# Expert weights of a mixture-of-experts layer consumed in two halves of the inner width

## The chip, the cores and the metric

The kernel runs on one core of one Trainium2 chip. The metric is device time in microseconds of one execution, as the median of three runs. A profile of one further execution gives the times of single instructions and transfers; all times below marked as positions are microseconds from the start of its span.

## What is computed

Two transformer layers over 256 tokens of width 1024, all in float32. Each layer has an attention mixer and then a mixture of 32 experts; a token goes to two experts of one group. The expert part, cut to what matters:

```
for e in range(N_EXPERTS):                       # 32 experts
    h = jax.nn.silu(xt @ w_gate[e]) * (xt @ w_up[e])   # 1024 -> 512, twice
    y = y + combine[:, e:e + 1] * (h @ w_down[e])      # 512 -> 1024
```

`w_gate`, `w_up` and `w_down` are 2 MB for each expert, so a layer's experts are 192 MB and the two layers' 384 MB.

## The kernel before

Experts are worked through in 16 pairs for each layer (`PAIRS`). The tokens of a pair are gathered into `xg` (64 slots for each expert), and the two experts stand side by side on TensorE: expert 0's 64 weight columns in one half of the array, expert 1's in the other, so that two matrix products stream at once. A float32 product shows in the trace as two MATMUL instructions.

The weights of a pair are 12 blocks of 1 MB (`CHUNKS`): four of gate, four of up, four of down, each block with its part of both experts. They lie in a ring of 16 places in SBUF (`places`), with six extra places for once in pair 3 (`once`). From pair 2 on SyncE issues them two at a time, 2 MB each (`two_chunks`), in the order in which TensorE uses them, and each issue waits until TensorE has released the places (`s_used`, `used_before`). `chunk_there` is TensorE's wait for a block.

A pair on TensorE (`pair`): the four gate blocks into PSUM bank 2 and the four up blocks into bank 3 (`up_chunk`, products of 512 columns), then two `scatter` products that add the previous pair's result `ye` to the tokens' sums, four transposes of `hid`, two more scatters, two transposes of `pickw` (the next scatter's selection), and then the four down blocks (`down_chunk`). Beside it ScalarE (`experts`) applies silu to the gate result, copies the next pair's tokens into `xg` in four copies (`ranges`), copies the turned hidden values to `hidT`, and copies half of `ye`; VectorE multiplies the up result by the silu (`hid`), copies `pickT` and the other half of `ye`. The first pair (`first_pair`) and the last (`last_pair`) have orders of their own; the last one puts its scatters between the gate and up blocks, works with `hid` in halves, and reads the last two down blocks column half by column half, so that the result's first half is ready sooner.

Layer 1 here is the first of the two, layer 2 the second. While the last blocks of layer 1 are used, the loads of layer 2's mixer (`w_in`, and `bias` out of `bounce`) are already queued behind them.

## Time and profile before

| | |
|---|---|
| median of 3 runs | 1183.36 us (1182.89 to 1183.46) |
| profiled execution | 1183.12 us, its span 1181.3 us |
| TensorE matmul busy | 1117.4 us (95% of the span) |
| VectorE, ScalarE, GpSimd busy | 237.0, 243.4, 168.5 us |
| read from HBM | 441.49 MB, 375 GB/s over the span |
| TensorE's idle time ahead of gate and up products | 46.2 us, most of it ended by a transfer of up or gate weights |
| mean granted TensorE clock | 0.996 |

The profiled execution is 0.24 us below the median of the runs. Busy times are unions over an engine's instructions; TensorE's ends are modelled, so its share does not say that it is at its peak. What waits for what is read from the idle times in the timeline and from the chain of work that ended last. The expert stages are the stretches from about 154 to 584 us and from about 738 to 1170 us.

### The profile page before, as it was taken

Reading aid. Unit: us, or ns where it says so; the run is one execution under the profiler, and the core shown is the slowest. Engines: PE = TensorE matmul, PEld = TensorE weight load, DVE = VectorE, ACT = ScalarE, POOL = GpSimd, SP = SyncE. Lnnn points to the kernel's source line nnn. Section 1 sums busy time; section 2 is a strip of 40 time slices with the busy share of each in tenths; the row PEclk is TensorE's granted clock in tenths of the full one; section 3 lists DMA queues with packets and bytes.
Section 4 is the critical chain, followed back from the end, with each engine's and each line's share of the span. In section 5 each row is a group of like instructions: output and inputs, shape, how many; then the busy total and the mean of one; then the engine's idle time right before and its main releaser. Section 6 shows DMA issues by size and latency. Waiting matters only on the chain.

```text
span 1181.3 us, 14644 instructions
## 1 busy us (share of the span) xinstructions
PE 1117.4 (95%) x5246; PEld 507.1 (43%) x5246; DVE 237.0 (20%) x637; ACT 243.4 (21%) x568; POOL 168.5 (14%) x347
## 2 busy tenths in 40 slices
PE   8999999999999888889999999999999998888897
PEld 6876543333333332323398856333333333333332
DVE  2864331000000000000145544300000000000002
ACT  2144251111211111111112233411211111111112
POOL 0003011111111111110046510211111111111100
PEclk9999999999999999999999999999999999999999
DMA  7985589999999999999998355899999999999994
GB/s 260 348 333 225 203 318 428 429 426 428 428 426 431 428 428 428 428 427 428 423 353 353 113 209 208 340 429 427 427 427 428 429 427 428 428 429 428 427 429 199
DMA packets 48590, 443.33 MB, mean 375 GB/s; under 512 B 9564, under 2 KB 14744, under 8 KB 16792
## 3 DMA queue, kind: packets, MB, share of 16 engines
q1 hardware_dynamic: 47464, 441.34, 90.0%
q10 hardware_dynamic: 1072, 1.26, 0.3%
q8 instruction: 35, 0.57, 0.2%
q14 instruction: 19, 0.16, 0.0%
HBM read 441.49 MB, written 1.09 MB: 375 GB/s over the span
## 4 chain that ended last, share of the span: by engine, by line
PE 67%; DMA 28%; ACT 2%; DVE 1%; issue 1%; ACTq 0%; SPq 0%; POOL 0%; DVEq 0%; POOLq 0%
PE PS L1671 24%; PE PS L1680 13%; DMA places<-in_moe_w_up 12%; DMA places<-in_moe_w_gate 11%; PE PS L1687 7%; PE PS L1555 5%; PE PS L1361 5%; PE PS L1423 4%; DMA places<-in_moe_w_down 3%; PE PS L1427 2%; PE PS L1435 1%; PE PS L1510 1%; DMA bias<-in_c_rel_bias 1%; PE PS L1539 1%; PE PS L1384 1%
## 5 line engine op out<-in xcount | busy, mean ns | idle before, releaser
L1671 PE MATMUL PS<-places,mix 128*64 128x512 f32 x1984 | 444.2, 597 | 46.2 <-DMA places<-in_moe_w_up 31.3
L1671 PEld LDWEIGHTS PS<-places,mix 128*64 128x64 f32 x1984 | 141.1, 137 | 340.6 <-issue 278.3
L1680 PE MATMUL PS<-places,gain_att 128*64 128x512 f32 x960 | 213.8, 596 | 0.8 <-ACT gain_att L861 0.5
L1687 PE MATMUL PS<-mix 128*128 128x512 f32 x256 | 124.8, 608 | 0.0
L826 ACT ACTIVATE mix<-acts 128x512 f32 x120 | 76.3, 636 | 229.7 <-PE PS L1671 217.3
L1680 PEld LDWEIGHTS PS<-places,gain_att 128*64 128x64 f32 x960 | 65.8, 137 | 124.5 <-issue 122.8
L574 POOL TENSOR_TENSOR sm<-sm 128x1 f32<-128x1 f32 x32 | 6.2, 193 | 692.9 <-PE PS L1762 660.3
L1279 DVE TENSOR_TENSOR mix<-PS,mix 128x512 f32<-128x512 f32 x28 | 19.4, 692 | 420.2 <-PE PS L1671 420.2
L633 POOL TENSOR_SCALAR mix<-drop 128x64 f32<-128x64 f32 x128 | 72.2, 584 | 0.0
L1687 PEld LDWEIGHTS PS<-mix 128*128 128x128 f32 x256 | 43.2, 189 | 60.0 <-issue 60.0
L873 ACT ACTIVATE mix<-PS 128x512 f32<-128x512 f32 x32 | 19.1, 598 | 236.8 <-PE PS L1680 224.9
L853 ACT ACTIVATE mix<-PS 128x512 f32<-128x512 f32 x32 | 19.1, 597 | 209.2 <-PE PS L1671 209.2
L1285 DVE COPY mix<-PS 128x512 f32<-128x512 f32 x32 | 22.1, 691 | 195.4 <-PE PS L1680 185.1
L1423 PE MATMUL PS<-acts,places 128*128 128x256 f32 x224 | 52.3, 386 | 0.0
L1423 PEld LDWEIGHTS PS<-acts,places 128*128 128x128 f32 x224 | 41.4, 190 | 8.3 <-issue 2.9
L1555 PE MATMUL PS<-places,mix 128*128 128x512 f32 x96 | 43.8, 598 | 0.0
L1361 PE MATMUL PS<-acts,places 128*128 128x128 f32 x336 | 40.5, 277 | 0.0
L1361 PEld LDWEIGHTS PS<-acts,places 128*128 128x128 f32 x336 | 38.8, 192 | 0.9 <-issue 0.7
L681 ACT ACTIVATE gain_att<-gain_att,sm 128x128 f32<-128x128 f32 (+1 forms) x64 | 28.5, 447 | 37.8 <-DVE sm L991 37.8
L1281 DVE COPY mix<-PS 128x256 f32<-128x256 f32 x32 | 13.6, 425 | 110.5 <-PE PS L1762 98.1
L690 ACT ACTIVATE gain_att<-PS 128x256 f32<-128x256 f32 (+2 forms) x32 | 14.4, 450 | 61.4 <-PE PS L1510 61.2
L1555 PEld LDWEIGHTS PS<-places,mix 128*128 128x128 f32 x96 | 17.3, 190 | 17.9 <-issue 17.9
(245 smaller groups left out, 801.0 us busy)
## 6 DMA issues: line engine op xcount, KB each, us to landing
places<-in_moe_w_gate SPq DMA_DIRECT2D x56, 2048.0 KB, 25.1
places<-in_moe_w_down SPq DMA_DIRECT2D x54, 2048.0 KB, 32.5
places<-in_moe_w_up SPq DMA_DIRECT2D x52, 2048.0 KB, 30.4
places<-in_moe_w_gate SPq DMA_DIRECT2D x16, 1024.0 KB, 10.9
places<-in_moe_w_up SPq DMA_DIRECT2D x16, 1024.0 KB, 6.5
places<-in_moe_w_down SPq DMA_DIRECT2D x16, 1024.0 KB, 7.4
places<-in_c_w_in SPq DMA_DIRECT2D x12, 1024.0 KB, 20.7
places<-in_ab_w_in SPq DMA_DIRECT2D x8, 1024.0 KB, 14.1
```

Of the source, the lines that this page charges most:

```text
L633: pool.tensor_scalar(pickw[:, t, e * SLOTS:(e + 1) * SLOTS], now_slots, now[:, t, e:e + 1], now_w[:, t, e:e + 1], ALU.is_equal, ALU.mult). ...
L681: act.activation(att[:, u % ATT, j, 0:n], att[:, u % ATT, j, 0:n], ACT.Exp, bias=nmax[:, u % ATT, j:j + 1], accum_out=den[:, 2 * u + j:2 * ...
L826: act.activation(dst[:, blocks, 0:SLOTS], src[:, blocks, 0:SLOTS], ACT.Copy).then_inc(s_xg[l], 1)
L1279: dve.tensor_tensor(hid, PS[:, 3], hid, ALU.mult).then_inc(s_hi[l], 1)
L1285: dve.tensor_copy(ye[:, 512:1024], PS[:, 7]).then_inc(s_yd[l], 1)
L1361: last = mm(PS[:, bank, m * P:(m + 1) * P], held, moved, start=(k == 0), stop=(k == 3))
L1423: last = mm(bank[0:m, half * SEQ:(half + 1) * SEQ], w[:, k, half * P:half * P + m], src[:, k, :], start=(k == 0), stop=(k == NK - 1))
L1427: last = mm(bank[:, half * CW:(half + 1) * CW], src[:, k, half * P:half * P + P], w[:, k, :], start=(k == 0), stop=(k == NK - 1))
L1555: last = mm(PS[:, OUT_BANK[q]], src[:, t * P:(t + 1) * P], wo[:, k // KPC, k % KPC, 512 * b:512 * b + 512], start=(m == 0), stop=(m == NK ...
L1671: last = mm(PS[e * SLOTS:(e + 1) * SLOTS, 2 + part, :], xg[:, k, e * SLOTS:(e + 1) * SLOTS], w[e][:, kk, :], start=(k == 0), stop=(k == NK ...
L1680: last = mm(PS[e * SLOTS:(e + 1) * SLOTS, 6 + b, :], hidT[:, k, e * SLOTS:(e + 1) * SLOTS], w[e][:, 512 * b:512 * b + 512], start=(k == 0) ...
L1687: last = mm(PS[:, Y_BANK[q]], pickT[:, t], ye[:, 512 * b:512 * b + 512], start=first, stop=final)
```

## The change

From the second pair on, the 512 inner columns of a pair are worked in two halves of 256. A half is two gate blocks, two up blocks, then, once its hidden values are made and turned, the two down blocks whose 256 rows belong to it. The weights are laid out anew by the host so that a 1 MB gate or up block holds four row groups of 256 columns instead of two of 512 (`halves`); bytes, transfer sizes and the number of transfers stay. The first pair keeps the old layout, which is appended as a seventeenth entry that only it reads. The last pair has the order of every other, with its last two down blocks still read column half by column half.

```diff
-            def block_of(c):
-                if c < 2 * UP_CHUNKS:
-                    return (w_gate, c) if c < UP_CHUNKS else (w_up, c - UP_CHUNKS)
-                return w_down, c - 2 * UP_CHUNKS
+            def block_of(i, c):
+                if i == 0:
+                    ...
+                return (w_gate, w_up, w_down)[c // 2 % 3], c // 6 * 2 + c % 2
...
 # ScalarE, experts()
-                    act.wait_ge(s_used[l], i * CHUNKS + UP_CHUNKS)
...
-                    if not first and not final:
-
-                        act.wait_ge(s_used[l], i * CHUNKS + 2 * UP_CHUNKS)
+                    for half in range(2):
+                        fs = slice(half * F // 2, (half + 1) * F // 2)
+                        ks = slice(half * NF // 2, (half + 1) * NF // 2)
+                        if not first:
+                            act.wait_ge(s_used[l], i * CHUNKS + half * CHUNKS // 2 + 2)
+                            act.wait_ge(s_ht[l], i * 2)
+                            act.activation(hid[:, fs], PS[:, 2, fs], ACT.Silu).then_inc(s_si[l], 1)
+                        act.wait_ge(s_ht[l], i * 2 + half + 1)
+                        act.activation(hidT[:, ks], PS[:, 2 + half if first else 2, fs].rearrange("p (k n) -> p k n", k=NF // 2),
+                                       ACT.Copy).then_inc(s_hT[l], 1)
+                    if not final:
                         ranges(entries, i * COPIES + FIRST_COPIES)
...
 # VectorE, experts()
+                    for half in range(2):
+                        fs = slice(half * F // 2, (half + 1) * F // 2)
+                        dve.wait_ge(s_used[l], i * CHUNKS + (2 * UP_CHUNKS if first else half * CHUNKS // 2 + 4))
+                        dve.wait_ge(s_si[l], i * 2 + half + 1)
+                        dve.tensor_tensor(hid[:, fs], PS[:, 3, fs], hid[:, fs], ALU.mult).then_inc(s_hi[l], 1)
...
 # TensorE
+                def up_chunk(i, n, rounds, c):
+
+                    half, part, rows = c // 6, c // 2 % 3, NK // 2
...
+                    for kk in range(rows):
+                        k = c % 2 * rows + kk
+                        for e in range(AT_ONCE):
+                            last = mm(PS[e * SLOTS:(e + 1) * SLOTS, 2 + part, half * F // 2:(half + 1) * F // 2],
+                                      xg[:, k, e * SLOTS:(e + 1) * SLOTS], w[e][:, kk, :], start=(k == 0), stop=(k == NK - 1))
...
+                def pair(i, n, rounds=0, second=False, final=False):
+
+                    for half in range(2):
+                        for c in range(6 * half, 6 * half + 4):
+                            up_chunk(i, n, rounds, c)
+                        if half == 0:
+                            ye_there(i - 1)
+                        scatter(2 * half, second)
+                        pe.wait_ge(s_hi[l], i * 2 + half + 1)
+                        for k in range(half * NF // 2, (half + 1) * NF // 2):
+                            last = nc.tensor.transpose(PS[:, 2, k * P:(k + 1) * P], hid[:, k * P:(k + 1) * P], ident)
+                        last.then_inc(s_ht[l], 1)
+                        scatter(2 * half + 1, second)
+                        if half == 1:
+                            pe.wait_ge(s_pw[l], i * PICKS + PICKS)
+                            for t in range(NT):
+                                last = nc.tensor.transpose(PS[:, 3, t * P:(t + 1) * P], pickw[:, t], ident)
+                            last.then_inc(s_pkt[l], 1)
+                        pe.wait_ge(s_hT[l], i * 2 + half + 1)
+                        if not (final and half):
+                            for k in range(half * NF // 2, (half + 1) * NF // 2):
+                                down_chunk(n, rounds, k)
```

How TensorE's instructions stand in one pair (here the second pair of a layer). Before: L1671 are the gate and up products, L1687 the scatters, L1756 and L1762 the transposes of `hid` and `pickw`, L1680 the down products; `xN` counts products (two MATMUL records each, one for a transpose).

```order
L1671 MATMUL PS<-places,mix 64x512 x32
L1687 MATMUL PS<-mix 128x512 x2
L1756 MATMUL PS<-acts,mix 128x128 x4
L1687 MATMUL PS<-mix 128x512 x2
L1762 MATMUL PS<-acts,mix 128x128 x2
L1680 MATMUL PS<-places,gain_att 64x512 x16
```

The same pair of the changed kernel, where L1677 are the gate and up products, L1696 the scatters, L1734 and L1740 the transposes and L1689 the down products:

```order
L1677 MATMUL PS<-places,mix 64x256 x32
L1696 MATMUL PS<-mix 128x512
L1734 MATMUL PS<-acts,mix 128x128 x2
L1696 MATMUL PS<-mix 128x512
L1689 MATMUL PS<-places,gain_att 64x512 x8
L1677 MATMUL PS<-places,mix 64x256 x32
L1696 MATMUL PS<-mix 128x512
L1734 MATMUL PS<-acts,mix 128x128 x2
L1696 MATMUL PS<-mix 128x512
L1740 MATMUL PS<-acts,mix 128x128 x2
L1689 MATMUL PS<-places,gain_att 64x512 x8
```

The 32 gate and up products of 512 columns have become 64 of 256, and each scatter and transpose stands between products of one half; the second half's up blocks are now followed by two scatters, two and two transposes and the last two down blocks.

TensorE at the end of a layer, before: the scatters lie between the blocks of the last pair, and between the last up block and the last two down blocks (L1722) stand the transposes of `hid` (L1707) and `pickw` (L1713) and the first two down blocks (L1680).

```order
L1671 MATMUL PS<-places,mix 64x512 x8
L1687 MATMUL PS<-mix 128x512
L1705 REGISTER_ALU
L1707 MATMUL PS<-acts,mix 128x128 x2
L1705 REGISTER_ALU
L1707 MATMUL PS<-acts,mix 128x128 x2
L1680 MATMUL PS<-places,gain_att 64x512 x4
L1711 REGISTER_ALU
L1713 MATMUL PS<-acts,mix 128x128 x2
L1680 MATMUL PS<-places,gain_att 64x512 x4
L1722 MATMUL PS<-places,gain_att 64x512 x8
L1687 MATMUL PS<-mix 128x512 x4
```

After, from the second half of the last pair on (L1752 are its last two down blocks; REGISTER_ALU rows work out the numbers that waits in the loop compare with):

```order
L1677 MATMUL PS<-places,mix 64x256 x32
L1696 MATMUL PS<-mix 128x512
L1732 REGISTER_ALU
L1734 MATMUL PS<-acts,mix 128x128 x2
L1696 MATMUL PS<-mix 128x512
L1738 REGISTER_ALU
L1740 MATMUL PS<-acts,mix 128x128 x2
L1752 MATMUL PS<-places,gain_att 64x512 x8
L1772 REGISTER_ALU
L1696 MATMUL PS<-mix 128x512 x4
```

The first two down blocks have left the place between the last up block and the last two down blocks, and two scatters have come there.

ScalarE in the second pair, before: silu (L853), four copies of the next pair's tokens (L826, one shown, each with the setting of its address), the copy to `hidT` (L871), half of `ye` (L873).

```order
L853 ACTIVATE mix<-PS 128x512
L826 ISA
L826 ACTIVATE mix<-acts 128x8x64
...
L871 ACTIVATE gain_att<-PS 128x512
L873 ACTIVATE mix<-PS 128x512
```

After: silu (L860) and the copy to `hidT` (L862) once for each half, then the four copies of tokens (L828, one shown), then half of `ye` (L870).

```order
L860 ACTIVATE mix<-PS 128x256
L862 ACTIVATE gain_att<-PS 128x256
L860 ACTIVATE mix<-PS 128x256
L862 ACTIVATE gain_att<-PS 128x256
L828 ISA
L828 ACTIVATE mix<-acts 128x8x64
...
L870 ACTIVATE mix<-PS 128x512
```

The four copies have moved from behind the silu, while TensorE does its scatters, to behind the second half's copy to `hidT`, when only the last two down blocks are left of the pair.

## Rows read from the trace of the kernel before

**Rows 1.** The page's 40 equal slices of the span: GB/s moved.
```profile
GB/s 260 348 333 225 203 318 428 429 426 428 428 426 431 428 428 428 428 427 428 423 353 353 113 209 208 340 429 427 427 427 428 429 427 428 428 429 428 427 429 199
```

**Rows 2.** Windows of one pair: stretch, length, busy by engine, TensorE clock, DMA share, GB/s.
```profile
180.22:205.26 25.04, 25.04 (x113) 8.92 (x111) 1.81 (x4) 4.22 (x7) 2.98 (x8) 1.00 1.01 428
467.00:496.30 29.30, 25.64 (x112) 8.74 (x110) 1.81 (x3) 4.22 (x7) 2.96 (x8) 1.00 1.00 428
```

**Rows 3.** Timeline of TensorE, late in layer 1: start, length, instructions, idle before.
```profile
471.57 3.65 PE L1671 MATMUL PS<-places,mix 128*64 128x512 f32 x16 [1.17 <-DMA places<-in_moe_w_gate]
476.57 3.65 PE L1671 MATMUL PS<-places,mix 128*64 128x512 f32 x16 [1.34 <-DMA places<-in_moe_w_up]
481.37 3.65 PE L1671 MATMUL PS<-places,mix 128*64 128x512 f32 x16 [1.15 <-DMA places<-in_moe_w_up]
```

**Rows 4.** Chain that ended last, in order of time, end of layer 1: start, us, what.
```profile
544.69 36.06 DMA places<-in_moe_w_down
580.89 3.65 PE PS L1722 x16
584.54 2.77 PE PS L1687 x6
```

**Rows 5.** Last down transfers: timeline of issues; issues by window (KB, us to landing).
```profile
539.87 5.15 SPq L501 DMA_DIRECT2D places<-in_moe_w_down  x2
places<-in_moe_w_down SPq DMA_DIRECT2D x1, 2048.0 KB, 36.0
...
1124.44 8.02 SPq L501 DMA_DIRECT2D places<-in_moe_w_down  x2
places<-in_moe_w_down SPq DMA_DIRECT2D x1, 2048.0 KB, 36.4
places<-in_moe_w_down SPq DMA_DIRECT2D x1, 2048.0 KB, 33.5
```

**Rows 6.** The same chain, end of layer 2.
```profile
1166.66 3.43 PE PS L1722 x16
```

**Rows 7.** The same chain: matmuls back to back, by line.
```profile
180.39 13.73 PE PS L1671 x64
...
638.69 0.37 PE PS L1539 x4
642.94 0.59 PE PS L1539 x8
```

**Rows 8.** The same chain, between a pair's up blocks and its down blocks.
```profile
455.66 1.91 PE PS L1687 x4
457.57 0.44 PE PS L1756 x4
458.01 1.72 PE PS L1687 x4
459.73 0.22 PE PS L1762 x2
```

**Rows 9.** Timeline, first pair of layer 1, where no scatter covers the hidden values.
```profile
171.87 0.77 PE L1735 MATMUL PS<-acts,mix 128*128 128x128 f32 x4 [0.53 <-DVE mix L1277]
172.78 1.94 PE L1680 MATMUL PS<-places,gain_att 128*64 128x512 f32 x8
```

**Rows 10.** Timeline of ScalarE in the third pair of layer 1.
```profile
219.30 2.96 ACT L826 ACTIVATE mix<-acts 128x512 f32 x4 [6.37 <-PE PS L1671]
```

**Rows 11.** Issues between 190.5 and 191 us: KB, us to landing.
```profile
places<-in_moe_w_down SPq DMA_DIRECT2D x1, 2048.0 KB, 15.9
```

**Rows 12.** Timeline, mixer of layer 2: VectorE and TensorE at the first scores.
```profile
616.63 0.91 DVE L940 MEMSET bias<- 64x1024 f32 x1 [1.51 <-DMA bias<-bounce]
618.05 0.49 PE L1435 MATMUL PS<-mix 64*128 64x128 f32 x4 [0.74 <-DVE gain_att L987]
```

**Rows 13.** Layer 2, last pair but one: timeline of TensorE, and a window after it.
```profile
1126.73 5.35 PE L1671 MATMUL PS<-places,mix 128*64 128x512 f32 x16 [2.33 <-DMA places<-in_moe_w_up]
...
1127.00:1128.00 1.00, 1.00 (x4) 0.24 (x2) 0.00 (x0) 0.00 (x0) 0.00 (x0) 0.50 1.15 492
```

More of the change, by code:

```diff
@@ L858, in experts @@
-                    for half in range(2 if first or final else 0):
-                        ks = slice(half * NF // 2, (half + 1) * NF // 2)
-                        act.wait_ge(s_ht[l], i + (1 if first else 2) + half)
-                        act.activation(hidT[:, ks], PS[:, 2 + half, half * F // 2:(half + 1) * F // 2].rearrange("p (k n) -> p k n", k=NF // 2),
-                                       ACT.Copy).then_inc(s_hT[l], 1)
-                    if first:
-                        ranges(entries, FIRST_COPIES)
+                        act.activation(hid, PS[:, 2], ACT.Silu).then_inc(s_si[l], 2)
@@ L1271, in experts @@
                 def experts(i, first=False, final=False):
[L1272 to L1279 removed]
+                    for half in range(2):
[3 more added lines that the diff above has]
+                        dve.tensor_tensor(hid[:, fs], PS[:, 3, fs], hid[:, fs], ALU.mult).then_inc(s_hi[l], 1)
                     dve.wait_ge(s_pkt[l], i + 1)
[L1281 removed]
+                    dve.tensor_copy(pickT, PS[:, 0 if first else 3, 0:NT * P].rearrange("p (t n) -> p t n", t=NT)).then_inc(s_pkT[l], 1)
                     if first:
@@ L1673, in up_chunk, with down_at @@
                     last.then_inc(s_used[l], 1)
+                def up_chunk(i, n, rounds, c):
+                    half, part, rows = c // 6, c // 2 % 3, NK // 2
+                    if c == 0:
+                        pe.wait_ge(s_xg[l], i * COPIES + FIRST_COPIES)
+                    if c == 2:
+                        pe.wait_ge(s_pkT[l], i)
+                    chunk_there(n, c, rounds)
+                    w = [slot(n, c, e).rearrange("p (k n) -> p k n", k=rows) for e in range(AT_ONCE)]
+                    for kk in range(rows):
[3 more added lines that the diff above has]
+                                      xg[:, k, e * SLOTS:(e + 1) * SLOTS], w[e][:, kk, :], start=(k == 0), stop=(k == NK - 1))
+                    last.then_inc(s_used[l], 1)
+                def down_at(n, k):
+                    return k // 2 * 6 + 4 + k % 2 if n else 2 * UP_CHUNKS + k
                 def down_chunk(n, rounds, k):
-                    chunk_there(n, 2 * UP_CHUNKS + k, rounds)
-                    w = [slot(n, 2 * UP_CHUNKS + k, e) for e in range(AT_ONCE)]
+                    chunk_there(n, down_at(n, k), rounds)
+                    w = [slot(n, down_at(n, k), e) for e in range(AT_ONCE)]
                     for b in range(2):
@@ L1694, in ye_there @@
                     pe.wait_ge(s_pkT[l], i + 1)
[L1696 to L1726 removed]
                 def first_pair():
                     for c in range(2 * UP_CHUNKS):
[L1731 removed]
+                        first_up_chunk(c)
                     for half in range(2):
@@ L1745, in first_pair @@
                             last.then_inc(s_pkt[l], 1)
-                def pair(i, n, rounds=0, second=False):
-                    for c in range(2 * UP_CHUNKS):
-                        up_chunk(i, False, n, rounds, c)
-                    ye_there(i - 1)
-                    scatter(0, second)
-                    scatter(1, second)
-                    pe.wait_ge(s_hi[l], i + 2)
-                    for k in range(NF):
-                        last = nc.tensor.transpose(PS[:, 2, k * P:(k + 1) * P], hid[:, k * P:(k + 1) * P], ident)
-                    last.then_inc(s_ht[l], 1)
-                    scatter(2, second)
-                    scatter(3, second)
-                    pe.wait_ge(s_pw[l], i * PICKS + PICKS)
-                    for t in range(NT):
-                        last = nc.tensor.transpose(PS[:, 3, t * P:(t + 1) * P], pickw[:, t], ident)
-                    last.then_inc(s_pkt[l], 1)
-                    pe.wait_ge(s_hT[l], i + 2)
-                    for k in range(NF):
-                        down_chunk(n, rounds, k)
+                def pair(i, n, rounds=0, second=False, final=False):
[19 more added lines that the diff above has]
+                                down_chunk(n, rounds, k)
+                    if final:
+                        for b in range(2):
+                            for k in range(NF // 2, NF):
+                                if b == 0:
+                                    chunk_there(n, down_at(n, k), rounds)
+                                for e in range(AT_ONCE):
+                                    last = mm(PS[e * SLOTS:(e + 1) * SLOTS, 6 + b, :], hidT[:, k, e * SLOTS:(e + 1) * SLOTS],
+                                              slot(n, down_at(n, k), e)[:, 512 * b:512 * b + 512], start=False, stop=(k == NF - 1))
+                            if b == 0:
+                                last.then_inc(s_left, 1)
+                        last.then_inc(s_used[l], NF // 2)
```

81 lines of the change are left out of this document (19 added, 62 removed).

## The prediction, written before the changed kernel ran

> **What bounds the kernel now.** I read the 40 slices of the page first, then windows of single pairs, then the timeline of TensorE, the chain of work that ended last, and at last the landing times of single transfers.
>
> The slices show the expert stages as a flat line: from about 177 us to the end of layer 1, and again in layer 2, 427 to 429 GB/s are moved, with a dip only around the mixer of layer 2 [rows 1]. A pair is 12 blocks of 1 MiB, 12.58 MB, which at 428 GB/s take 29.4 us. TensorE needs less: an early pair, whose weights were all there, took 25.04 us; a late one took 29.30 us, of which it was busy 25.64 [rows 2]. The early pairs run ahead on stored weights, but the transfers go at 428 GB/s under them as well; once the store is used up, TensorE waits for gate and up blocks some 1.2 to 1.3 us at a time, three times a pair [rows 3]. So an expert stage ends when its bytes are through, plus what TensorE still has to do after the last landing. In layer 1 that landing is at 580.9, and TensorE, which had waited for it, does the last two down blocks in 3.65 us and goes on to the last scatters [rows 4]. In layer 2 the last down transfer is issued at 1132.1 (1124.44 + 8.02, less 0.33 of issuing) and lands 33.5 us later, at 1165.6 [rows 5]; TensorE reaches those blocks at 1166.66, one us late [rows 6]. Part of its lateness is a block that took 5.35 us instead of 3.65, after a wait of 2.33 us, with the granted clock at 0.50, which is 1.2 GHz of 2.4 [rows 13].
>
> **The change part by part.** Bytes, transfer sizes and their number stay the same, so the 29.4 us of a pair stay.
>
> *Narrower products.* Each pair has 64 gate and up products of 256 columns for 32 of 512, 128 MATMUL records for 64. The row for the old ones: 64 in 13.73 us, 214.5 ns each, two streaming side by side [rows 7]. No row has 256 columns on half the array. The nearest has 128 columns there: 4 records in 0.37 us and 8 in 0.59, so four more cost 0.22 us, 55 ns each [rows 7]. Streaming alone would be a quarter of 213 ns (512 columns at 2.4 GHz), 53.3 ns, so a record costs 1.7 ns beyond it. For 256 columns I take 106.7 + 1.7 = 108.4 ns: a block pair of 32 records takes 3.47 us where 16 took 3.43, +0.04 us, and a pair of experts +0.15. Lower bound nothing; upper bound 224 ns a record, if halving the columns saved nothing. I stay with the 55 ns row, because it is the same tiling and shorter still. What hides the +0.15 is the idle time of 3.7 us a pair [rows 2, 3]; in the last pair, one block pair lies after the last up landing, so +0.04 in each layer shows.
>
> The page of the Trainium skill "TensorE: Matmul & The Clock Gate", section Part 3 on packing small matmuls, says that a weight load overlaps a running matmul only when it is for other rows of the array. Here both experts use all 128 rows, so by that rule loads would add to streaming. These rows speak against it: 64 records would have to take longer than the 13.65 us of pure streaming by more than the 0.08 they do.
>
> *Covers of the small steps.* In a half, the multiplication by silu has one scatter as its cover. Without any cover TensorE waited 0.53 us for it [rows 9]; a scatter is 3.63/4 = 0.91 us [rows 8]. The copy to `hidT` is covered by a scatter too; from the start of the transposes to the first down product it took 0.91 us bare, and that with four transposes instead of two [rows 9], against 0.22 + 0.91. So both are covered, by 0.2 us at the least, and I cost them at nothing. Were the cover gone, up to 0.5 us twice a pair would still go into the 3.7 us of idle time, and only the last pair's would show.
>
> *The copies of tokens.* The next pair's first gate block waits for them (L826, now L828), and behind them in ScalarE's queue stands only half of `ye`. They take 2.96 us [rows 10]. They now start with the second half's `hidT`, about 0.6 us before the last down blocks, which take 3.5 us; so they end about 1.1 us before TensorE wants them. Cost nothing; late next, if they were slower, would be the first gate block.
>
> *Release of places.* SyncE's issues keep their order and their count per pair. Down blocks of the first half are released earlier in the pair, and the gap without a release is now two scatters, the transposes and two down blocks, 2.2 + 3.5 us, where four scatters stood before. In the first full pair the third release comes about 2.5 us later than before. A transfer issued there took 15.9 us to land, that is, three were queued [rows 11], so the transfers don't run dry. Cost nothing.
>
> *The end of layer 1.* This is where the order matters. Before, the last-but-one transfer was down (issued 539.87, landed 36.0 later, at 575.9 [rows 5]), and the up blocks had come 4.9 us before that, so TensorE could be through with `hid` when the last down blocks landed. Now the transfer that lands at 575.9 is the second half's up. After it come its products, 3.65 + 0.04 us [rows 3], then two scatters (3.63/2), two transposes (0.22) and two of `pickw` (0.22), 2.25 us [rows 8]. The last down blocks start at 575.9 + 3.69 + 2.25 = 581.84 instead of 580.89: +0.95 us. The tail behind (3.65 us, then the last scatters) is as before [rows 4].
>
> *What of it reaches layer 2.* The mixer of layer 2 waits once for a transfer: VectorE for the bias until 616.63, idle 1.51 us, and TensorE behind it for 0.74 us [rows 12]. That load lies in the queue behind bytes that come no later than before. A start 0.95 later loses its 0.74 us of waiting there: +0.21 remains, and moves all of layer 2.
>
> *The end of layer 2.* The up blocks of the second half land where the first down did, at 1124.44 + 36.4 = 1160.8 [rows 5]; + 3.69 + 2.25 = 1166.8 against 1166.66: +0.1 us. TensorE's lateness there is used up by the new order's own.
>
> Sum: 0.21 + 0.1 = +0.3 us, with +0.1 for the small steps inside, on the profiled 1183.12; on the median, 1183.36, it makes 1183.8. A measurement of this kernel tells 0.2% (2.4 us) from no change.
>
> **The rivals.**
> *Slower: TensorE becomes the bound.* If a record of 256 columns cost as much as one of 512, a pair would take 25.04 + 64 x 0.2145 = 38.8 us, and 30 pairs at 38.8 instead of 29.4 at most some 280 us more, about 1460. It decides from 25.04 + 4.3 us a pair on, that is from 141 ns a record. Against it: 55 ns for 128 columns. 3 in 100. By the skill's rule above, with 0.14 us for each load of two added, it would be about 34 us a pair; I give that no chance beside these 3.
> *Slower: the covers fail in the last pairs.* Both waits bare (0.5 us each) in both last pairs, +2 us, and a block at 1.2 GHz, as there was one, in a place from which nothing is regained, +1.7 us: with the +0.4 of the sum, 1187.5. It becomes more than 0.2% once one of them comes on top of the other. For it: the up blocks are now the last thing but one, with a DMA wait ahead of them. 9 in 100.
> *Faster: the transfers themselves go faster.* Nothing else can give 2.4 us: the two last landings bound the tails, and removing every wait after them gains 1 us in layer 2. Blocks are now released soon after they land, so the queue may be more even; it would take 0.3% of the some 830 us of transfers (28 slices of 29.5 us at full rate [rows 1]), 1180.9. Against it: the rate is flat from early pairs, with three transfers queued, to late ones with seven [rows 1, 2, 11]. 6 in 100.
> *No change of its own, only the tails as worked out:* 82 in 100.
>
> **How the numbers follow.** The likeliest case gives 1183.8, its own range 1182.2 (a tail without a step at 1.2 GHz and a lower median) to 1185.7 (both tails +0.95, nothing absorbed by the bias wait). With half of the second slower rival taken in, the range is 1181.9 to 1186.6. Faster by over 0.2%: 0.06; within: 0.82; slower: 0.12, from the same cases.
>
> **What would show it.** Pairs early in a stage at 25.1 to 25.3 us; late ones at 29.3 to 29.4 with 428 GB/s, and TensorE waiting for gate and up blocks, no longer three times in a row but once or twice each half, and never for ScalarE's copies. MATMUL records of 256 columns at 107 to 112 ns when back to back. The last two down blocks of layer 1 start about one us after their landing, where they waited for it before, and TensorE's wait for the bias is gone or near it. Layer 2's last two down blocks start about 1.2 us after their landing. The prediction is wrong if the record of 256 columns costs over 141 ns, if TensorE waits for ScalarE or VectorE inside a pair by more than its idle time, or if the GB/s of the slices is other than 427 to 429.

## The result

| | before | changed |
|---|---|---|
| median | 1182.58 us (1181.98 to 1183.72, 10 runs) | 1185.64 us (1184.39 to 1188.18, 10 runs) |
| ratio | | 1.0024, 95% interval 1.0015 to 1.0033 |
| profiled execution, its span | 1183.12, 1181.3 us | 1185.47, 1183.7 us |

The change makes the kernel 3.1 us slower, a little more than the 0.2% named in the prediction. A second comparison of the same two gave 1.0026 (1.0017 to 1.0035). (The ratio in the table and its interval are worked out from all ten runs of each, not from the two medians alone, whose quotient is 1.0026.) The 1185.64 us lie inside the forecast range, 1181.9 to 1186.6, but the likeliest case was +0.4, so some 2.7 us are missing from the sum.

The page's row of the instruction queue (packets, MB, share), before:

```profile
q8 instruction: 35, 0.57, 0.2%
```

The page of the changed kernel, the rows of the moved rates, of the instruction queue and of the gate and up products:

```profile
GB/s 242 343 354 213 202 333 429 427 423 427 428 427 429 429 429 428 428 427 426 423 351 349 114 207 213 342 427 427 420 427 429 427 426 432 427 426 431 424 429 195
...
q8 instruction: 46, 0.75, 0.3%
...
L1677 PE MATMUL PS<-places,mix 128*64 128x256 f32 x3712 | 416.9, 380 | 36.9 <-DMA places<-in_moe_w_up 29.2
```

The line of rates is nearly as flat as before [rows 1]: in layer 2 the thirteen slices from the 27th to the 39th run from 420 to 432, mean 427.1, where before they ran from 427 to 429, mean 427.9. TensorE still waits for up and gate transfers. What is new on the page is the 46: eleven more packets of 16 KB that carry instructions.

Windows of one pair, early and late in layer 1 (columns as in [rows 2]):

```profile
180.64:206.10 25.46, 25.46 (x177) 13.29 (x174) 1.95 (x5) 4.56 (x10) 2.97 (x8) 1.00 1.01 428
467.00:496.30 29.30, 26.31 (x176) 12.91 (x174) 1.96 (x4) 4.56 (x9) 2.92 (x9) 1.00 1.01 428
```

The early pair, bound by TensorE, took 25.46 us for 25.04. The late window is cut at the same two times as in [rows 2], so its length says nothing; what it shows is the same 428 GB/s, with 0.67 us more of work inside. By the starts in the timelines, from the first gate products of one pair to those of the next, a late pair took 29.36 us before and 29.43 changed:

```profile
466.80 3.60 PE L1671 MATMUL PS<-places,mix 128*64 128x512 f32 x16
...
496.16 3.64 PE L1671 MATMUL PS<-places,mix 128*64 128x512 f32 x16
```

```profile
467.73 3.67 PE L1677 MATMUL PS<-places,mix 128*64 128x256 f32 x32 [0.17 <-DMA places<-in_moe_w_gate]
...
497.16 3.21 PE L1677 MATMUL PS<-places,mix 128*64 128x256 f32 x27 [0.26 <-DMA places<-in_moe_w_gate]
```

The chain that ended last, an early block group and then the ends of both layers:

```profile
180.43 6.91 PE PS L1677 x64
...
575.90 3.67 PE PS L1677 x32
581.93 3.58 PE PS L1752 x16
585.51 2.77 PE PS L1696 x6
...
1162.95 3.67 PE PS L1677 x32
1168.97 3.58 PE PS L1752 x16
1172.56 2.79 PE PS L1696 x6
```

64 records in 6.91 us are 108.0 ns each. In layer 1 the last two down blocks start at 581.93, 1.04 us later than in [rows 4] (TensorE's scatters start at the same distance behind them, 585.51 against 584.54: +0.97). In layer 2 they start at 1168.97 against 1166.66 [rows 6], +2.3.

Timeline at the bias load of layer 2: its issue, and VectorE's wait for it.

```profile
587.70 1.14 SPq L519 DMA_DIRECT2D bias<-bounce  x1
...
617.70 0.91 DVE L937 MEMSET bias<- 64x1024 f32 x1 [1.61 <-DMA bias<-bounce]
```

The bias came 1.07 us later than in [rows 12], and the wait for it is no shorter: 1.61 for 1.51 us.

**Where the 2.4 us between the two spans lie.** I cut both executions at six points: the first expert transfer issued after 150 us, the last landing, the end of the last down product, and the same in layer 2 (from 735 us on).

| us | before | changed | difference |
|---|---|---|---|
| start to first issue | 156.47 | 156.51 | +0.04 |
| layer 1, first issue to last landing | 424.28 | 424.24 | -0.04 |
| last landing to end of last down product | 3.79 | 4.76 | +0.97 |
| to layer 2's first issue (end, mixer, routing) | 156.54 | 156.64 | +0.10 |
| layer 2, first issue to last landing | 424.57 | 425.61 | +1.04 |
| last landing to end of last down product | 4.45 | 4.80 | +0.35 |
| rest | 11.17 | 11.11 | -0.06 |

Two single executions cannot settle single microseconds: such cuts differ by up to one us between executions of one kernel, as the runs below show. So each candidate was made alone and timed.

### The profile page after: what moved, and what is told of

It reads as the page before. It is cut to its first block, busy times and chain, and to the rows that moved or that the text cites. A ratio compares the mean times of both kernels' runs of the same rounds, so it can differ in the third digit from the quotient of the medians.

```text
span 1183.7 us, 18752 instructions
## 1 busy us (share of the span) xinstructions
PE 1129.1 (95%) x7166; PEld 642.6 (54%) x7166; DVE 241.5 (20%) x665; ACT 253.3 (21%) x626; POOL 168.4 (14%) x347
## 4 chain that ended last, share of the span: by engine, by line
PE 71%; DMA 24%; DVE 2%; ACT 2%; issue 1%; ACTq 0%; POOL 0%; DVEq 0%; POOLq 0%
PE PS L1677 23%; DMA places<-in_moe_w_up 23%; PE PS L1689 14%; PE PS L1696 8%; PE PS L1417 5%; PE PS L1549 5%; PE PS L1355 5%; PE PS L1421 2%; PE PS L1429 1%; PE PS L1661 1%; PE PS L1504 1%; PE PS L1533 1%; PE PS L1734 1%; PE PS L1402 1%; PE PS L1378 1%
## 5 line engine op out<-in xcount | busy, mean ns | idle before, releaser
L1677 PE MATMUL PS<-places,mix 128*64 128x256 f32 x3712 | 416.9, 380 | 36.9 <-DMA places<-in_moe_w_up 29.2
L1677 PEld LDWEIGHTS PS<-places,mix 128*64 128x64 f32 x3712 | 269.5, 137 | 203.2 <-issue 43.6
L1689 PE MATMUL PS<-places,gain_att 128*64 128x512 f32 x960 | 219.2, 598 | 0.3
L1273 DVE TENSOR_TENSOR mix<-PS,mix 128x256 f32<-128x256 f32 x64 | 27.0, 424 | 617.0 <-PE PS L1677 602.5
L1696 PE MATMUL PS<-mix 128*128 128x512 f32 x256 | 136.5, 618 | 0.0
L1689 PEld LDWEIGHTS PS<-places,gain_att 128*64 128x64 f32 x960 | 63.5, 136 | 129.9 <-issue 110.1
L860 ACT ACTIVATE mix<-PS 128x256 f32<-128x256 f32 x60 | 23.0, 383 | 335.9 <-PE PS L1677 327.6
L862 ACT ACTIVATE gain_att<-PS 128x256 f32<-128x256 f32 x64 | 24.4, 383 | 293.8 <-PE PS L1734 283.1
L828 ACT ACTIVATE mix<-acts 128x512 f32 x120 | 76.0, 633 | 12.4 <-ACT mix L828 0.5
L1696 PEld LDWEIGHTS PS<-mix 128*128 128x128 f32 x256 | 38.8, 189 | 27.1 <-issue 27.1
L683 ACT ACTIVATE gain_att<-gain_att,sm 128x128 f32<-128x128 f32 (+1 forms) x64 | 28.5, 447 | 37.9 <-DVE sm L988 37.9
L1734 PEld LDWEIGHTS PS<-acts,mix 128*128 128x128 f32 x120 | 16.7, 140 | 32.0 <-DVE mix L1273 23.5
L1661 PE MATMUL PS<-places,mix 128*64 128x512 f32 x128 | 29.8, 601 | 1.9 <-ACT mix L844 1.9
L870 ACT ACTIVATE mix<-PS 128x512 f32<-128x512 f32 x32 | 19.1, 597 | 54.7 <-PE PS L1689 49.6
```

Of the source, the lines that this page charges most:

```text
L683: act.activation(att[:, u % ATT, j, 0:n], att[:, u % ATT, j, 0:n], ACT.Exp, bias=nmax[:, u % ATT, j:j + 1], accum_out=den[:, 2 * u + j:2 * ...
L828: act.activation(dst[:, blocks, 0:SLOTS], src[:, blocks, 0:SLOTS], ACT.Copy).then_inc(s_xg[l], 1)
L1273: dve.tensor_tensor(hid[:, fs], PS[:, 3, fs], hid[:, fs], ALU.mult).then_inc(s_hi[l], 1)
L1661: last = mm(PS[e * SLOTS:(e + 1) * SLOTS, 2 + part, :], xg[:, k, e * SLOTS:(e + 1) * SLOTS], w[e][:, kk, :], start=(k == 0), stop=(k == NK ...
L1677: last = mm(PS[e * SLOTS:(e + 1) * SLOTS, 2 + part, half * F // 2:(half + 1) * F // 2], xg[:, k, e * SLOTS:(e + 1) * SLOTS], w[e][:, kk, : ...
L1689: last = mm(PS[e * SLOTS:(e + 1) * SLOTS, 6 + b, :], hidT[:, k, e * SLOTS:(e + 1) * SLOTS], w[e][:, 512 * b:512 * b + 512], start=(k == 0) ...
```

## The experiments

All ratios are to the kernel before in the same comparison. What the profiles of all of them give at the disputed places, in us (bias: from layer 1's last expert landing to VectorE's MEMSET that waits for the bias; wait: its idle time there; tail: from the last landing to the end of the last down product; layer 1, layer 2: from the first expert transfer's issue to the last landing; fetches: packets in the row q8 instruction). For b2, whose pairs are much longer, only the first columns are given:

```
                   ratio   95% interval      fetches  layer 1  tail 1  bias   wait  layer 2  tail 2
before                                          35     424.28    3.79  35.88  1.51  424.57    4.45
changed            1.0024  1.0015 - 1.0033      46     424.24    4.76  36.95  1.61  425.61    4.80
a1_after_again     1.0026  1.0017 - 1.0035      46     424.47    4.74  35.89  0.57  425.65    4.79
a2_late_downs      1.0015  1.0006 - 1.0024      46     423.74    3.70  36.90  2.62  425.53    3.70
a3_new_end_alone   1.0008  0.9998 - 1.0018      36     422.99    4.74  35.98  0.67  425.09    4.80
a4_narrow_alone    1.0019  1.0010 - 1.0028      46     424.10    3.79  37.06  2.70  425.45    3.79
b1_waits_128       1.0002  0.9993 - 1.0011      46     423.74    3.79  36.97  2.60  425.07    3.79
b2_waits_256       1.2465  1.2449 - 1.2482      76
b3_quarters        1.0067  1.0055 - 1.0080      90     428.20    3.79  35.72  1.35  429.54    3.79
b4_before_again    1.0004  0.9995 - 1.0013      35     423.48    3.79  36.40  2.04  425.77    3.79
c1_split_last      1.0008  0.9995 - 1.0020      35     423.91    3.19  36.02  2.25  424.51    3.22
c2_narrow_again    1.0011  1.0002 - 1.0021      46     424.01    3.79  36.97  2.60  425.64    3.79
c3_waits_again     1.0013  1.0002 - 1.0023      46     424.19    3.79  36.61  2.25  425.34    3.79
d1_split_and_early 1.0005  0.9995 - 1.0014      35     423.03    3.08  36.44  2.79  424.79    3.31
```

**The change again**, with no edit.

> The changed kernel once more, as the reference for the runs beside it. All theories: 2 to 4 us above the kernel before, as in its first ten runs (+3.06). Its profile tells how much of the +1.05 us that layer 2's transfers took longer in the first profile is chance: if it is chance, layer 2 from the first block of the first pair to the landing of the second half's up weights takes 412.8 us here and not 413.9.

Measured: 1185.19 us, 1.0026. Its profile has the two late tails, as the first, but the bias one us earlier and a wait of 0.57 us only. Layer 2's transfers took 425.65 us again, so by the sign given above their extra microsecond would not be chance; the kernel before, run again below, then took 425.77.

**The new order with the old end.** The changed kernel, where only the last pair uses gate, up, gate, up of its halves first and then all four down blocks:

```diff
-                        for c in range(6 * half, 6 * half + 4):
-                            up_chunk(i, n, rounds, c)
+                        for c in range(4 * half if final else 6 * half, (4 * half if final else 6 * half) + 4):
+                            up_chunk(i, n, rounds, c, final)
```

> The changed kernel, but in the last pair of each layer the first half's two down blocks are loaded and used after the second half's up blocks. Theory T (the end of a layer costs 1 us in each layer, because up weights land last but one): about 2 us below the changed kernel, so 1 us above the kernel before; the last two down blocks of layer 1 start within 0.3 us of their landing. Theory P (the loss is spread over all pairs, by the narrower products, the order or the transfers): no more than 0.5 us below the changed kernel.

Measured: 1184.00 us, 1.0015. Both last blocks start at their landing again (tails 3.70). About 1.3 us of the 3.1 are gone, where Theory T expected 2 and Theory P at most 0.5; the rest stays with the 46 fetches.

**The new end alone.** The kernel before, where only the last pair has the new order and layout:

```diff
+            def final_block_of(c):
+                return (w_gate, w_up, w_down)[c // 2 % 3], c // 6 * 2 + c % 2
...
-                src, j = block_of(c)
+                src, j = final_block_of(c) if final else block_of(c)
```

> The kernel before, but the last pair of each layer has the new order and layout. Theory T: 2 us above the kernel before (1184.6), the last two down blocks of layer 1 start 0.9 to 1.0 us after they could have, and layer 2's mixer is 1 us late. Theory P: within 0.5 us of the kernel before.

Measured: 1183.54 us, 1.0008 (0.9998 to 1.0018), about +0.9. Its chain at the end of both layers:

```profile
573.49 3.67 PE PS L1737 x32
...
579.52 3.58 PE PS L1777 x16
...
1165.14 3.58 PE PS L1777 x16
```

The last blocks start over one us after their landings, at 578.37 and 1163.93, in both layers, tails 4.74 and 4.80: twice +0.95 to +1.0 against 3.79. Timed, only about half of that appears, between the two theories; the interval, -0.2 to +2.1 us, excludes neither none nor both. The wait for the bias, 0.67 us here, suggests why the end of layer 1 counts for little; the last part comes back to it.

**Narrower products alone.** The kernel before, every gate and up product of pairs 1 to 15 as two of 256 columns, blocks and order unchanged:

```diff
-                        for e in range(AT_ONCE):
-                            last = mm(PS[e * SLOTS:(e + 1) * SLOTS, 2 + part, :], ..., start=(k == 0), stop=(k == NK - 1))
+                        for cols in [slice(0, F)] if first else [slice(0, F // 2), slice(F // 2, F)]:
+                            for e in range(AT_ONCE):
+                                last = mm(PS[e * SLOTS:(e + 1) * SLOTS, 2 + part, cols], ...)
```

> The kernel before, its blocks and their order untouched, but each gate and up product of pairs 1 to 15 is issued as two of 256 columns. Theory T: within 0.5 us of the kernel before; early pairs take 25.1 to 25.2 us instead of 25.04. Theory P, if the narrower products are what costs: 2 to 3 us above. Both expect 108 ns for a record of 256 columns back to back.

> The kernel before with each gate and up product of pairs 1 to 15 as two of 256 columns, once more, beside the kernel with idle waits. Theory F (each added fetch of instructions takes a DMA engine for 1.06 us, the narrower products cost nothing else): 46 fetches in place of 35, transfers of a layer longer by about 0.5 us each, the time the same as that of the kernel with idle waits within 0.5 us, both about 1.0 to 1.3 us over before. Theory N (the narrower products cost something of their own): this one 2.0 us or more over before, the one with waits within 0.5 us of before.

Measured: 1.0019, and 1.0011 in a second comparison, +1.3 to +2.2 us with no block or order moved and both ends as before. So about half of the loss, perhaps more, appears without the halves' order. The early pair took 25.11 us (180.21 to 205.32), as expected; the other 0.35 us of the changed kernel's 25.46 come with the order.

**Idle instructions alone.** Waits that are satisfied long before, in TensorE's stream. Two waits make one instruction, so these are 8 ahead of each four records and 128 a pair, as many as the narrower products bring:

```diff
                     for kk in range(KPU):
+                        for n_wait in range(0 if first else 16):
+                            pe.wait_ge((s_blank, s_wrg)[n_wait % 2], 1)
```

> The kernel before, with 128 more instructions for each pair in TensorE's stream that do nothing: waits on semaphores long reached, eight ahead of each row group of the gate and up products of pairs 1 to 15. That is as many instructions as the 32 products of 256 columns and their weight loads add. The run with narrower products alone was 2.24 us above the kernel before though its last down blocks started at their landing. Theory I (more instructions mean more 16 KB instruction fetches among the weight transfers, 46 instead of 35, and these delay the transfers): 46 fetches here as well, and 1.5 to 3 us above the kernel before. Theory W (the narrower products themselves, by TensorE's pace): within 0.5 us of the kernel before.

> The kernel before with 128 waits that are long satisfied put in TensorE's stream in each of pairs 1 to 15, once more: as many instructions as the narrower products bring. Theory F: 46 fetches, about 1.0 to 1.3 us over before, as the kernel with narrower products. Theory N: within 0.5 us of before.

Measured: 1.0002 and 1.0013, 46 fetches both times. The mean of these two, 1.0008, and that of the two runs of narrower products, 1.0015, have intervals of some 0.0007 to either side, so they are not told apart: neither the theory that the products cost something of their own is excluded, nor the one that fetches are all. b1 by itself, 1.0002, is what Theory W expected; c3 is nearer to Theory F. The transfers speak for a price of the fetches, as Theory F expected of them (about 0.5 us a layer): the two layers' stretches in the table add up to 847.8 to 849.3 us in the five profiles with 35 or 36 packets, mean 848.5, and to 848.8 to 850.1 us in the seven with 46, mean 849.5.

**Twice the idle instructions.** 32 waits instead of 16 at each place, 256 instructions a pair.

> The same with 256 idle instructions for each pair. Theory I: 57 fetches, 3 to 6 us above the kernel before. Theory W: within 0.7 us of the kernel before, unless the waits themselves make TensorE's sequencer the bound, which would show as pairs of over 29.4 us.

Measured: 1475.21 us, 1.2465 (1.2449 to 1.2482). The timeline of TensorE in layer 1:

```profile
460.09 1.08 PE L1673 MATMUL PS<-places,mix 128*64 128x512 f32 x4 [0.67 <-issue]
461.83 1.08 PE L1673 MATMUL PS<-places,mix 128*64 128x512 f32 x4 [0.67 <-issue]
```

Four records every 1.74 us, with 0.67 us in which no transfer and no engine is waited for: its sequencer was the bound. As a timed test of fetches it says nothing, since the transfers no longer fill the kernel; it gives the price of the waits, below. But it had 76 packets where 57 were expected, which matters for the next run.

**Four products of 128 columns.** As the narrower products, in quarters.

> The kernel before with each gate and up product of pairs 1 to 15 issued as four of 128 columns: 384 more instructions for each pair, 33 more fetches. Theory I: about three times the 2.24 us of the halved products, 5 to 8 us above the kernel before. Theory W: early pairs 25.3 to 26 us instead of 25.04, late ones 29.3 as ever, and within 1 us of the run with halved products, so 2 to 3 us above.

Measured: 1191.67 us, 1.0067, +8 us, as Theory I expected, though with 55 more fetches and not 33. The early pair took 25.28 us. The page's row of instruction packets:

```profile
q8 instruction: 90, 1.47, 0.5%
```

In a window of 115 us in the middle of layer 1, 360 to 475, the kernel before has no packet of instructions at all, nor has the changed one; here there are ten. First the queues' rows of the kernel before, then with quarters:

```profile
q1 hardware_dynamic: 3385, 49.27, 100.6%
```

```profile
q1 hardware_dynamic: 3359, 48.87, 100.1%
q8 instruction: 10, 0.16, 0.6%
```

With the ten packets, 0.40 MB less of weights moved, which at 428 GB/s are 0.9 us.

TensorE's loop runs over four pairs. The Trainium skill's page "Runtime: NRT & Kernel Launch", section "Instruction fetch mechanics", says that TensorE holds 2048 instructions and is refilled in blocks of 256. With 256 to a packet, the loop's body can be estimated: early in layer 1 of the kernel before one packet came every 28.5 us, so 225 instructions to a pair of 25 us and some 900 to the body; 1,400 with 128 more a pair, 1,900 with the 256 waits, 2,400 with quarters. The traces show that the first two stay on the chip from one turn of the loop to the next (no packet for 130 us or more in layer 1), and that the other two are fetched at every turn. So the limit lies between 1,400 and 1,900 by this estimate. Room for 2048 fits three of the four; the body of 1,900 is a little below it and did not stay, and no run here tells why. Nor does the section say that a loop stays; it calls the fetching purely sequential, and here the measurement decides. It also calls the cost of a refill mostly hidden, which here holds for TensorE and not for the transfers.

What a packet costs: in the trace it holds a DMA engine for 1.06 us (95.6 us in all for 90, 37.3 for 35), a weight packet of the same size 0.61. Packets of weights are no longer than before, 0.613 or 0.614 us in the median in each of these kernels, so the narrower products' reads don't slow them. And the packets do not seem to be spread over all 16 engines. Windows of the last microseconds of layer 2's transfers, first of the kernel before (b4), then with quarters; the last two columns are the DMA engines' share and GB/s:

```profile
1159.00:1161.00 2.00, 2.00 (x9) 0.59 (x6) 0.31 (x1) 0.00 (x0) 0.00 (x0) 1.00 0.96 410
1161.00:1163.00 2.00, 1.74 (x10) 0.84 (x10) 0.44 (x2) 0.66 (x2) 0.00 (x0) 1.00 0.73 311
1163.00:1165.00 2.00, 2.00 (x10) 0.54 (x8) 0.36 (x1) 0.00 (x0) 0.00 (x0) 1.00 0.14 57
```

```profile
1164.00:1166.00 2.00, 1.96 (x22) 1.13 (x23) 0.00 (x0) 0.00 (x0) 0.00 (x0) 1.00 0.94 401
1166.00:1168.00 2.00, 2.00 (x40) 2.00 (x38) 0.00 (x0) 0.00 (x0) 0.00 (x0) 1.00 0.63 270
1168.00:1170.00 2.00, 2.00 (x18) 1.17 (x14) 0.76 (x2) 0.07 (x1) 0.00 (x0) 1.00 0.49 205
1170.00:1172.00 2.00, 1.75 (x9) 0.49 (x8) 0.00 (x0) 0.59 (x2) 0.00 (x0) 1.00 0.51 213
1172.00:1174.00 2.00, 2.00 (x12) 0.69 (x10) 0.42 (x1) 0.00 (x0) 0.00 (x0) 1.00 0.27 115
```

Before, the share falls from full to nearly nothing in 4 us. With quarters it stands at a half for 4 us and more: half of the engines are through, the other half work on alone. I read this as the half that the instructions went to; the trace's views don't name the engine of a packet. Counting how many packets of the traces are open at a time in the last 9 us before layer 2's last landing bears it out: with quarters six to nine were open for 6.2 us, with 46 fetches and the old order for 1.9 to 2.4 us (both runs with narrower products and both with waits alike), with 46 and the changed order for 1.1 to 1.7, and in the five profiles with 35 or 36 for 0.3 to 0.9. As an estimate, 55 more packets of 1.06 us on eight engines would be 7.3 us; layers 1 and 2 took 3.8 to 5.0 us more each in this profile than in the two of before, and the timed difference is 8. For the 11 packets of the change the same estimate gives 1.5 us, against the 0.9 and 1.8 us of the two means above.

**The kernel before again**, in the same comparison.

> The kernel before itself, for a second profile beside the others and as a measure of what two sets of runs of one kernel differ by. All theories: a ratio of 1.000 within 0.0006, and both expert stages' transfers, from the first released block to the last landing, of 423 to 425.1 us.

Measured: 1183.51, 1.0004 (0.9995 to 1.0013): what the same kernel differs from itself by. Its second layer took 425.77 us, longer than the changed kernel's and over the 425.1 expected; its first took 423.48, 0.8 less than in the first profile. So the +1.04 of the table of cuts is no evidence by itself.

**Can the end of before be shortened?** Its last transfer of 2 MB issued as two of 1 MB, and the last products taken block by block:

```diff
+                if final and c == CHUNKS - 2:
+                    for one in range(2):
+                        sp.dma_start(places[:, p + one, :], src[l, bass.ds(pair, 1), j // 2, :, one]...).then_inc(s_place[l][p + one], 16)
+                    return
...
-                    for b in range(2):
-                        for k in range(NF // 2, NF):
+                    for k in range(NF // 2, NF):
...
+                        for b in range(2):
```

> The kernel before, with the last transfer of each layer (2 MB, the down blocks of k 2 and 3 of the last pair) issued as two of 1 MB, and the last 16 product records taken block by block (8 for k 2, then 8 for k 3). Theory A (in the kernel before a layer ends with the last landing, and what TensorE still has to do after it is what counts): 8 records of 228 ns remain after the landing instead of 16, the time from the last landing to the last product falls from 3.79 to about 2.0 us in both layers, and the run takes 3.6 us less, about 0.997 of before. Rival B (the smaller packets cost what the shorter end gives, or the two halves land together, since the 16 DMA engines end up to 3 us apart): the time from the landing to the last product stays above 3 us, or the last landing comes over 1 us later, and the run is within 0.1% of before.

Measured: 1183.06 us, 1.0008 (0.9995 to 1.0020); no gain, Rival B's numbers, though not for its reasons: the two halves landed 2.5 us apart (576.75 and 579.22 in layer 1). The tail fell to 3.2, not 2.0. The timeline of TensorE:

```profile
564.66 3.65 PE L1686 MATMUL PS<-places,mix 128*64 128x512 f32 x16 [0.88 <-DMA places<-in_moe_w_up]
...
569.41 3.65 PE L1686 MATMUL PS<-places,mix 128*64 128x512 f32 x16
...
574.81 1.94 PE L1695 MATMUL PS<-places,gain_att 128*64 128x512 f32 x8 [0.26 <-ACT gain_att L876]
...
578.81 3.60 PE L1739 MATMUL PS<-places,gain_att 128*64 128x512 f32 x16
```

After the wait of 0.88 us for the last-but-one up transfer TensorE does not wait for a transfer again. Its own chain reaches the last two blocks at 578.81, 0.4 us before the very last landing. So when the last landing stops being the bound, the tail falls by 0.6 us only (3.79 to 3.19): close behind it lies the bound that the changed kernel's end has, the work behind the up blocks.

**And with the last pair's scatters earlier**, so that this chain is shorter:

```diff
-                        if c % 2:
-                            scatter(c // 2)
+                        for q in {1: (0, 1), 3: (2,), 5: (3,)}.get(c, ()):
+                            scatter(q)
```

> The kernel with the split last transfer, and the four scatter products of the last pair moved one step earlier: two after the first gate transfer's blocks, one after the second's, one after the first up transfer's, none after the last up blocks. Theory C (with the last transfer split, a layer ends with TensorE's own chain behind the last up landing, 3.65 of products, 1.06 of scatter, 0.9 of turns, 4.2 of down blocks, 3.43 of the last ones, and the scatter is the piece that can go): the last products end 2.2 to 2.4 us after the last landing in both layers, in place of 3.2 with the split alone and 3.79 before; 2.9 us less than before, a ratio of about 0.9975. Rival D (the two scatters after the first gate blocks make the later blocks late, or the landing of the second last MB is itself what counts): the time from the last landing to the last product stays at 3.0 us or more, and the run is within 0.1% of before.

Measured: 1183.01 us, 1.0005 (0.9995 to 1.0014); tails 3.08 and 3.31. The same place:

```profile
565.11 3.65 PE L1686 MATMUL PS<-places,mix 128*64 128x512 f32 x16
...
569.75 3.65 PE L1686 MATMUL PS<-places,mix 128*64 128x512 f32 x16
574.02 0.77 PE L1722 MATMUL PS<-acts,mix 128*128 128x128 f32 x4 [0.62 <-DVE mix L1292]
574.93 1.94 PE L1695 MATMUL PS<-places,gain_att 128*64 128x512 f32 x8
```

The scatter that was removed had covered VectorE's multiplication: a wait of 0.62 us stands in its place. And the last two up blocks started no earlier than with the split alone (at 569.75, and at 569.41 with the split alone, the last landing being 0.24 us later here). Rival D's numbers came. Neither kernel beats the one before.

## Why the prediction was near, and what it missed

**Transfers bound the kernel, TensorE does not become the bound:** right. A late pair took 29.4 us as before (the 29.30 of [rows 2] is the length of the window). **A record of 256 columns at 108.4 ns:** 108.0. **The early pair at 25.1 to 25.3:** 25.46, over the range; the block groups gave the +0.1 expected, the other 0.3 lies between them, and layer 1's transfers took no longer for it (424.24 us for 424.28).

**Covers, copies of tokens, TensorE never waiting for ScalarE inside a pair:** right; the waits left are for up (29.2 us) and gate transfers.

**"The last down blocks start at 575.9 + 3.69 + 2.25 = 581.84":** 581.93. Of the +0.95, **"+0.21 remains"** after the bias wait. The pair of profiles seemed to refute this, since the bias came a microsecond later too. The other profiles bear it out. In the three executions with the new end the wait was 1.61, 0.57 and 0.67 us, in ten with a tail of 3.8 or less 1.35 to 2.79; and the bias arrives 35.7 to 37.1 us after the last expert landing, whichever end the layer has. So a later start of the mixer only eats into VectorE's wait, of some 2.3 us in the mean. What is left of the lateness can be read further on. From the MEMSET behind the bias to layer 2's first expert issue it took 124.44 to 124.47 us in four profiles with the old end (before, b1, b3, c2) and 124.45, 124.58 and 124.48 in the three with the new one; in the six others, none with the new end, 125.7 to 126.0. So no more than about 0.1 us of the +0.21 came, and layer 1's late end hardly reached layer 2. The end of layer 1 alone was not timed.

**"The end of layer 2: +0.1":** the step that failed first. The new end's own part was right: its last blocks were forecast about 1.2 us after their landing and started 1.21 us after it (1168.97 and 1167.76). But it was worked out against 1166.66, where the kernel before was one us late in the one profiled execution, after a block at a granted clock of 0.50. In that execution TensorE did not wait for a transfer again from that block to the end, so nothing took the lateness away. That is no property of the kernel: in the other executions with its end (a4, b1, b3, b4, c2, c3) the tail is 3.79 us in layer 2 as well. The new end has 4.79 to 4.80 in all three. The term is +1.0 and not +0.1, and nothing behind it absorbs it; a3's +0.9 is about that.

**"Bytes, transfer sizes and their number stay the same, so the 29.4 us of a pair stay":** the other step that failed. The bytes of the instructions did not stay: 35 packets became 46, and the sum had no term for them. The size is the mean of the four comparisons with 46 fetches and the old end, 1.0011, or +1.3 us with some 0.6 to either side. That this many instructions in TensorE's stream go with a loss is shown by quarters above all (+8 us for 55 packets, and the half of the engines that ended late), by one of the two runs with waits, and by the longer transfers in the seven profiles with 46 packets. That the narrower products cost nothing of their own beside it stays open.

Sum of what was measured alone: +0.9 for the end, +1.3 to +1.8 for the number of instructions (the mean of all four, and that of the two with narrower products), 2.2 to 2.7 us of the 3.1, inside the intervals of about 1 us. Whether the order of the releases in the halves costs the transfers something is open too: in layer 2 the three profiles with the changed order lie at 425.5 to 425.7 us, the nine others without quarters at 424.5 to 425.8.

**The range held by luck.** Its upper part was built from two late tails that both count and from failed covers. Neither came: only the tail of layer 2 counted, no cover failed, and the instruction packets, which the sum did not have, made up the rest. Its own range, up to 1185.7, also counts a part twice: the 1183.8 already holds 0.3 us of the tails, so two tails of 0.95 make 1185.4, which the measured 1185.64 passes. The outcome just over 0.2% had been given 12 in 100, and one of the prediction's own signs of being wrong came: slices other than 427 to 429, though the kernel before has such slices as well.

**The rivals.** None came. The slower ones had the right sign with the wrong mechanism: no cover failed, and the block at 1.2 GHz made the kernel before late, not the changed one.

## What to carry to other kernels

When transfers fill a kernel, its instructions ride in the same engines. Count them before splitting products, and watch whether a loop still fits: about 1,400 instructions stayed, about 1,900 and 2,400 were fetched at every turn. A stage that is bound by its last landing has, behind that, the chain from the last-but-one landing as its next bound; work out how far away it is (0.6 us here) before moving work there or hoping to gain by splitting the last transfer. A lateness in one profile that goes with a dip of the clock is not to be entered in a sum as a property of the kernel.

## What the runs showed of the hardware

- A 16 KB packet of instructions holds a DMA engine 1.06 us; a weight packet of the same size, 0.61 us.
- TensorE's loop bodies of about 900 and 1,400 instructions caused no fetch for 130 us or more; bodies of about 1,900 and 2,400 did so all the time (35 or 46 packets in a run, against 76 and 90).
- With 90 such packets, the DMA engines' share stood near a half from 1168 to 1172 us, before the last landing at 1174.6; with 35 it fell from 0.96 to 0.14 within three windows of 2 us.
- Instructions that only hold satisfied waits are not free in TensorE's stream. Eight ahead of four records brought no wait for the sequencer. With 16, the four came every 1.74 us instead of 0.86: at most 0.11 us for each.
- MATMUL records of 128 by 256 with a 64-column weight load each ran at 108.0 ns back to back, so the loads lay beside streaming, as in [rows 7].
- The 2 MB of bias, gathered from `bounce`, landed 28.7 to 30.5 us after their issue in thirteen profiles.
